# Half 0 of the output projection woven into the last head or pair of two layers of a four-layer trunk

## What is computed

```python
def mla_mixer(h, w_in, q_norm_g, kv_norm_g, w_uq, w_ukv, w_out, cos, sin):    # layer 1, 16 heads
    c_q, c_kv, k_rope, g = split(h @ w_in)
    q, k_nope, v = rmsnorm(c_q) @ w_uq, *(rmsnorm(c_kv) @ w_ukv)     # rotary parts apart
    ...
    p = softmax(where(causal, (q_nope @ k_nope + q_rope @ k_rope) * scale, -inf))
    return ((p @ v) * silu(g)) @ w_out                               # w_out 2048 x 1024
def sb_mixer(h, w_in, w_out):                                        # layer 2, 16 heads of 64
    z = (q @ k) * scale
    log_beta, log_1m_beta = log_sigmoid(z), where(strict, log_sigmoid(-z), 0)
    after = cumsum(log_1m_beta, reverse=True) - log_1m_beta
    a = where(strict, exp(log_beta + after), 0)
    return ((a @ v) * silu(g)) @ w_out                               # w_out 1024 x 1024
```

## Time and profile before

| | |
|---|---|
| median of 3 runs | 2589.19 us |
| lowest, highest | 2583.03, 2590.29 us |
| the profiled execution | 2590.05 us |
| its span in the trace | 2588.1 us |
| mean granted TensorE clock over the span | 0.968 |
| DMA | 160.31 MB, mean 62 GB/s |
| end of the last `pv` of the latent layer | about 1337.7 us |
| end of the last `pv` of stick-breaking | about 2039.9 us |

### The profile page before, as it was taken

The page is one execution under the profiler, slowest core; times in us unless marked ns, Lnnn a source line. Parts: engine busy times, 40 slices in busy tenths (PEclk is TensorE's granted clock), DMA queues, the critical chain, the costliest instruction groups (busy, mean ns, idle before and its releaser), DMA issues. The chain is left out here.

```text
span 2588.1 us, 43259 instructions
## 1 busy us (share of the span) xinstructions
PE 2365.7 (91%) x17364; PEld 1335.5 (52%) x17364; DVE 1569.3 (61%) x2220; ACT 1348.4 (52%) x2029; POOL 462.5 (18%) x418
## 2 busy tenths in 40 slices
PE   8999989987888888989888999999998799999987
PEld 4667654444544454445444455555454345776643
DVE  5566665765655556656546566666666465667654
ACT  4434443445545444444433677777778543444432
POOL 0000111122111102011012223233223210011011
PEclk9999999998899999999989999999999899999998
DMA  3011112214334334424331221121211121111113
GB/s 116 26 42 50 34 34 91 75 48 89 74 75 83 77 79 79 86 65 95 80 86 57 59 58 34 50 58 50 58 41 34 41 91 34 35 50 33 34 59 120
DMA packets 197721, 160.31 MB, mean 62 GB/s; under 512 B 160114, under 2 KB 161394, under 8 KB 197524
## 3 DMA queue, kind: packets, MB, share of 16 engines
q1 hardware_dynamic: 193428, 153.35, 22.4%
q0 software_dynamic: 4096, 4.20, 0.7%
HBM read 98.79 MB, written 4.19 MB: 40 GB/s over the span
## 5 line engine op out<-in xcount | busy, mean ns | idle before, releaser
L240 PE MATMUL psum<-h_hi,w_hi 128*128 128x512 f16 x1128 | 431.7, 383 | 35.7 <-ACT mla_silu_g L285 18.4
L241 PE MATMUL psum<-h_lo,w_hi 128*128 128x512 f16 x1128 | 431.5, 382 | 0.0
L242 PE MATMUL psum<-h_hi,w_lo 128*128 128x512 f16 x1128 | 431.3, 382 | 0.0
L2340 DVE SCALAR_TENSOR_TENSOR w_lo<-wf,w_hi 128x1024 f16<-128x1024 f32 (+3 forms) x194 | 231.1, 1199 | 138.8 <-ACT w_hi L2335 138.7
L256 PE MATMUL psum<-w_hi,h_hi 128*128 128x128 f16 x1504 | 256.9, 219 | 0.0
L258 PE MATMUL psum<-w_hi,h_lo 128*128 128x128 f16 x1504 | 256.5, 219 | 0.0
L257 PE MATMUL psum<-w_lo,h_hi 128*128 128x128 f16 x1504 | 256.5, 219 | 0.0
L1619 ACT ACTIVATE ssum<-psum,mla_neg_top 128x128 f32<-128x128 f32 (+7 forms) x128 | 94.7, 740 | 298.3 <-DVE mla_neg_top L1526 298.3
L1097 POOL TENSOR_TENSOR sb_al<-sb_zc,sb_ah 128x256 f16<-128x256 f32 (+2 forms) x96 | 166.2, 1732 | 373.0 <-ACT sb_ah L1062 373.0
L2335 ACT ACTIVATE w_hi<-wf 128x1024 f16<-128x1024 f32 (+3 forms) x194 | 187.0, 975 | 39.7 <-PE psum L242 19.6
L240 PEld LDWEIGHTS psum<-h_hi,w_hi 128*128 128x128 f16 x1128 | 111.3, 99 | 159.1 <-issue 42.9
(11 more groups left out here) (325 smaller groups left out, 5859.7 us busy)
## 6 DMA issues: line engine op xcount, KB each, us to landing
wf<-in_gla_out SPq DMA_DIRECT2D x32, 512.0 KB, 3.5
wf<-in_sb_in SPq DMA_DIRECT2D x32, 512.0 KB, 3.5
wf<-in_mla_out SPq DMA_DIRECT2D x20, 512.0 KB, 3.9
wf<-in_gla_v SPq DMA_DIRECT2D x16, 512.0 KB, 3.5
wf<-in_gla_g SPq DMA_DIRECT2D x16, 512.0 KB, 3.5
wf<-in_mla_gate SPq DMA_DIRECT2D x16, 512.0 KB, 3.6
wf<-in_sb_out SPq DMA_DIRECT2D x16, 512.0 KB, 3.5
xT<-in_x_T SPq DMA_DIRECT2D x16, 256.0 KB, 5.1
```

What stands on the lines that cost most here:

```text
L240: pe.matmul(out, wh[:, w], act_hi[:, k, tok], start=(i == 0), stop=False)
L241: pe.matmul(out, wh[:, w], act_lo[:, k, tok], start=False, stop=False)
L242: mm = pe.matmul(out, wl[:, w], act_hi[:, k, tok], start=False, stop=(i == last))
L2340: dve.scalar_tensor_tensor(out=self.w_lo[s % Layer.NSPLIT][:, 0:cols], in0=self.wf[s % Layer.NLOAD][:, 0:cols], scalar=W_SCALE, in1=self.w ...
```

## The change

In both layers the eight final output units of half 0 leave the tail for the attention's last head or pair. In the latent layer they stand from block i = 5 of the last head (`OUT_CLOSES`), three of them opened, and all are done ahead of the last `pv`; behind it stand `ns` 0 and then two opened units of half 1. In stick-breaking three units are opened from step 3 of the last pair (`OUT_FROM`) and the rest is woven from step 6 (`HALF_DONE`); one unit of half 1 is opened before the last `pv`, one behind it. The opened units wait for half 0 of the head outputs alone. The squares of half 0 move from ScalarE to GpSimd (`pool_half=0`), and in the latent layer its sums are kept in the tile `st_hi`, since `ssum` is still in use. The latent layer's table puts the norm pieces one unit earlier.

```diff
@@ class Residual
-    def __init__(self, layer, sq):
+    def __init__(self, layer, sq, pool_half=None, rows=None):
...
     def act(self, act, n):
...
-        if not final:
+        if not final or c == self.pool_half:
             return
...
     def pool(self, pool, n):
...
+        s = self.rows[c]
+        if c == self.pool_half:
+            x = L.net.xT[:, k, c * HALF:(c + 1) * HALF]
+            L.wait_unit(pool, n)
+            pool.tensor_tensor(s if k == 0 else self.sq[k % 2], x, x, ALU.mult).then_inc(self.pool_sq_ready, 1)
+            pool.wait_ge(self.pool_sq_ready, k + 1)
+        if k == 0:
+            return
...
         pool.tensor_tensor(s, s, self.sq[k % 2][:], ALU.add).then_inc(self.sum_ready, 1)
@@ class StickBreaking
+    OUT_FROM, HALF_DONE = 3, 6
+    OPENED = 3
...
-            self.resid = Residual(L, [self.zc[0][:, 0, :], self.zc[0][:, 1, :]])
+            self.resid = Residual(L, [self.sg[:, 0, 0:HALF], self.sg[:, 0, HALF:T]], pool_half=0)
@@ def build_items
+                if p == final and i == self.OUT_FROM:
+                    out = []
+                    for k in range(KD):
+                        out += L.slab(w_out[k], 1024, [("x", (k, 0, True))], self.out_banks(k, 0))
+                    filler, out = L.open_early(L.cut(out, ("x",)), self.OPENED)
+                    items += main
+                if p == final and i == self.HALF_DONE:
+                    items += weave(main, filler, lambda it: it[0] == "part")
+                    filler, main = out, []
...
-        early, last = L.open_early(L.cut(last, ("x",)), 2)
-        items += weave(main, early, lambda it: it[0] == "part")
-        items += [("pv", self.PAIRS * len(self.STEPS) - 1)] + last
+        for k in range(KD):
+            last += L.slab(w_out[k], 1024, [("x", (k, 1, True))], self.out_banks(k, 1))
+        first, last = L.open_early(L.cut(last, ("x",)), 1)
+        second, last = L.open_early(last, 1)
+        items += weave(main, filler, lambda it: it[0] in ("u", "part"))
+        items += first + [("pv", self.PAIRS * len(self.STEPS) - 1)] + second + last
@@ def pe
-                pe.wait_ge(self.yl_ready, 2 * (L.share(n, part, KD)[-1] + 1))
+                pe.wait_ge(self.yl_ready, 2 * L.share(n, part, KD)[-1] + c + 1)
@@ class LatentAttention
-            self.resid = Residual(L, [self.rt[0], self.rt[1]])
+            self.resid = Residual(L, [self.rt[0][:], self.rt[1][:]], pool_half=0,
+                                  rows=[self.st_hi[:].bitcast(F32), net.ssum[:, HALF:T]])
...
+    BEHIND = {0: [("nk", 0, 0)], 1: [("nk", 0, 1), ("nk", 0, 2)], 2: [("nk", 0, 3), ("nk", 0, 4)],
+              3: [("nk", 0, 5), ("nk", 0, 6)], 4: [("nk", 0, 7), ("gw", 0)], 5: [], 6: [("gw", 1)]}
+    END = [("gu", 0, 0), ("gw", 2), ("ns", 1)] + Handover.REST
+    OUT_CLOSES = 5
@@ def build_items
-            if i == TT - 1:
+            if h + 1 == MLA_HEADS and i == self.OUT_CLOSES:
+                opened, out = L.open_early(L.cut(self.last_out(0), ("x",)), 3)
+                items += weave_even(main, L.cut(filler, ("x", "g")) + opened, self.pe_cost)
+                main, filler = [], out
+            elif i == TT - 1 and h + 1 < MLA_HEADS:
...
-        early, tail = L.open_early(L.cut(tail, ("x",)), 3)
-        items += early + [("pv", last)] + tail
+        main += [("gap", 2), ("pv", last)]
+        items += weave_even(main, filler, self.pe_cost)
+        early, tail = L.open_early(L.cut(self.last_out(1), ("x",)), 2)
+        items += [("ns", 0)] + early + tail
```

More of the change, by code:

```diff
@@ L353, in __init__ @@
         self.wait_sums, self.wait_slab = wait_sums, wait_slab
+        self.rows = [net.ssum[:, self.half(c)] for c in range(2)]
         self.gain = net.gains[:, coming.gain, :]
@@ L393, in pe @@
                 self.rsqrt.wait_done(pe, 0)
-            pe.matmul(self.bank(c), net.ones[:], net.ssum[:, self.half(c)], start=True,
-                      stop=True).then_inc(self.total, 1)
+            pe.matmul(self.bank(c), net.ones[:], self.rows[c], start=True, stop=True).then_inc(self.total, 1)
         elif kind == "gu":
@@ L549 @@
 class Residual:
-    def __init__(self, layer, sq):
+    def __init__(self, layer, sq, pool_half=None, rows=None):
         L = self.layer = layer
-        self.sq = sq
+        self.rows = rows or [layer.net.ssum[:, c * HALF:(c + 1) * HALF] for c in range(2)]
+        self.sq, self.pool_half = sq, pool_half
         self.sq_ready, self.sum_ready = L.sem("sq_ready"), L.sem("sum_ready")
+        self.pool_sq_ready = L.sem("pool_sq_ready")
     def dve(self, dve, n):
@@ L571, in act @@
         if k == 0:
-            out = L.net.ssum[:, c * HALF:(c + 1) * HALF]
+            out = self.rows[c]
         else:
@@ L587, in pool @@
     def pool(self, pool, n):
-        _, (k, c, final, *_), _, _ = self.layer.units[n]
-        if not final or k == 0:
+        L = self.layer
+        _, (k, c, final, *_), _, b = L.units[n]
+        if not final:
             return
-        s = self.layer.net.ssum[:, c * HALF:(c + 1) * HALF]
-        pool.wait_ge(self.sq_ready, c * KD + k + 1)
+        s = self.rows[c]
[6 more added lines that the diff above has]
+            return
+        if c != self.pool_half:
+            pool.wait_ge(self.sq_ready, (c if self.pool_half is None else 0) * KD + k + 1)
         if k > 1:
@@ L820, in build_items @@
         last = []
-        for c in range(2):
-            for k in range(KD):
-                last += L.slab(w_out[k], 1024, [("x", (k, c, True))], [5, 6, 7])
-        early, last = L.open_early(L.cut(last, ("x",)), 2)
-        items += weave(main, early, lambda it: it[0] == "part")
-        items += [("pv", self.PAIRS * len(self.STEPS) - 1)] + last
+        for k in range(KD):
[4 more added lines that the diff above has]
+        items += first + [("pv", self.PAIRS * len(self.STEPS) - 1)] + second + last
         L.finish_items(self.handover.placed(self.place_products(items), L.units))
@@ L1090, in pool @@
         elif kind == "u":
-            if L.units[a[0]][0] == "x":
+            name, payload, _, _ = L.units[a[0]]
+            if name == "x":
+                if payload[:2] == (1, 0):
+                    pool.wait_ge(self.yt_ready, 2 * (self.PAIRS - 1))
                 self.resid.pool(pool, a[0])
@@ L1191, in __init__ @@
                                      self.wait_out_slab)
+            self.handover.rows = self.resid.rows
+            self.handover.BEHIND, self.handover.END = self.BEHIND, self.END
             self.crs = Rsqrt(L, "latent")
@@ L1323, in build_items, with last_out @@
             main += [("gap", 1)]
[L1324 to L1331 removed]
+        main += [("gap", 2), ("pv", last)]
+        items += weave_even(main, filler, self.pe_cost)
+        early, tail = L.open_early(L.cut(self.last_out(1), ("x",)), 2)
+        items += [("ns", 0)] + early + tail
+        L.finish_items(self.handover.placed(self.place_gates(items), L.units))
+    def last_out(self, c):
+        out = []
+        for part in range(4):
+            out += self.add_units([self.out_slab(MLA_HEADS // self.GROUP - 1, part, (c,))], [0, 0])
+        return out
     def place_gates(self, items):
@@ L1637, in act @@
                                ACT.Copy).then_inc(self.yh_ready, 1)
-    def act_x(self, act, n):
-        k, c, final, group = self.L.units[n][1]
-        if final and (k, c) in ((1, 0), (2, 0)):
-            act.wait_ge(self.rlo, len(self.ropes))
-        self.resid.act(act, n)
     def pool(self, pool, kind, *a):
@@ L1682, in pool @@
         elif kind == "u":
-            if L.units[a[0]][0] == "x":
+            name, payload, _, _ = L.units[a[0]]
+            if name == "x":
+                if payload[:3] == (0, 0, True):
+                    for even_odd in range(2):
+                        pool.wait_ge(self.stacked[even_odd], 256 * (MLA_HEADS // 4))
                 self.resid.pool(pool, a[0])
@@ L2320, in __init__ @@
         self.w_lo_done = ctx.enter_context(nc.semaphore("w_lo_done"))
+        self.queries_staged = [ctx.enter_context(nc.semaphore(f"queries_staged{i}")) for i in range(2)]
         self.guests_from = 0
```

20 lines of the change are left out of this document (9 added, 11 removed).

## The result

| | before | changed |
|---|---|---|
| median | 2589.10 us (4 runs) | 2558.12 us (4 runs) |
| lowest, highest | 2583.03, 2590.29 | 2556.61, 2560.41 |
| the profiled execution, its span | 2590.05, 2588.1 | 2556.61, 2554.9 |
| mean granted clock | 0.968 | 0.977 |

The account below looks back on a forecast made before the run. TensorE, busy 91% of a 2588.1 us span, was taken as the bound. Gains of 17.3 us in stick-breaking and 11.2 in the latent layer made 28.5: 2561.6 profiled, 2560.7 on the median, stated as 2561; range 2546 to 2577.

Parts of the forecast that it names:

- The waits (steps 1, 2, 4 and 6): Stick-breaking's last pair: filled waits +17.9 us, six later matmuls -1.3, step loop longer than TensorE's work -3.5, GpSimd-VectorE interference -2.1.
- Step 6: Stick-breaking: VectorE and GpSimd block each other; two new squares hit a w_lo inside the loop, costing 2.1 us.
- Step 3, the clock: Stick-breaking's last pair and tail: TensorE's slow clock goes, gaining 6.3 us; 1.2 near the first wait stays.
- Step 5: Stick-breaking: GpSimd's `al`, sum and square take 4.7 to 5.2 of 8.4 us per step, so covered.
- Step 1: Latent layer's last head: 69 matmuls (14.9 us) move ahead of the last pv's end, which comes only 7.0 us later.
- Step 2: Latent layer, last pv to last output slab's w_lo: 15.7 us, with half 0's sum matmul waiting 4.2 for GpSimd.
- Step 3: Latent layer, last output slab's w_lo to half 1's sum matmul: one update moves ahead, a 1.64 wait goes; 24.6 us.
- Everything covered: Rival: stick-breaking's step loop hides itself and the latent sums are ready at the last pv's end; 2551 us, chance 0.14.
- The port everywhere: Rival: all 16 squares GpSimd takes over cost 1.07 us each through the port shared with VectorE; 2576, chance 0.10.
- The latent layer gives nothing: Rival: latent head gains turn into the wait at the sum matmul, leaving 17.3 us alone; 2572, chance 0.15.
- Lock-step: Rival: in stick-breaking unit and chain alternate, no wait is filled and the clock falls; slower, 2610 us, chance 0.04.
- It does nothing: Rival: gaps close at one place and open at the next; 2589 us, chance 0.03.

Follow-up runs that it names:

- e5: Changed kernel with six slab splits in stick-breaking's last pair moved behind the next step's subtraction and low half of L; 2556.4 us, 0.9868 of the kernel before.
- e2: Stick-breaking as changed, latent layer as in the kernel before; 2570.7 us, 0.9931 of the kernel before.
- e3: Changed kernel, but in the latent layer half 0's sum matmul stands behind unit 0 of half 1 and norm pieces one unit later, as before; 2560.7 us.
- e7: Changed kernel, but stick-breaking's squares of half 0 are back on ScalarE; 2564.5 us, 0.9901 of the kernel before.
- e9: Changed kernel with half 0's latent sum matmul behind two opened units, second guest slab split later, and stick-breaking's slab splits behind the step; 2552.9 us.
- e8: Changed kernel, but in the latent layer the second guest slab is split behind unit 7 of half 1, not ahead of it; 2559.4 us.
- e1: Latent layer as changed, stick-breaking as in the kernel before; 2580.1 us, 0.9969 of the kernel before.

## Why the prediction was right

The forecast was 28.2 us on the median (2589.2 to 2561); 31.0 came. In the profiled execution 2.1 us lie ahead of P, where nothing was changed, which is luck. The sum of 28.5 for the two places stands against 29.9 measured there if the latent layer is read at Z (9.6 + 20.3), and 31.5 if at C, where the prediction read it (11.2 + 20.3).

**Stick-breaking, 17.3 forecast, 20.3 measured.**
- *The waits (steps 1, 2, 4 and 6)*: 17.9 - 1.3 - 3.5 - 2.1 = 11.0 forecast; TensorE's idle time fell by 11.9. The first wait for L stayed at 2.7 and the six matmuls' 1.3 came, both to the tenth. The loop's regular step was 8.96 us where 9.1 was reckoned, its three waits were 3.3, and e5 took them away and gained 3.2. The price of 3.5 was met with the wrong make-up: TensorE's own step is 8.65 and not 8.4, so a regular step loses 0.3, and the rest falls on the first full-width step and on the one with two slabs. That one took 10.08 us, over the 10 that the prediction gave as a sign of being wrong, and the next made up for it with 6.68.
- *Step 6* was sized too high. Three `w_lo` ahead of a subtraction took 1.33, 1.44 and 1.96 us where 1.23 was reckoned, together 1.0 more and not 2.1, and that is already in the 3.3 of the loop's waits. The largest hit, the `Ll` of 2.28 at 2005.30, shows no price: the step with it took 8.96 us and the next one, without, 8.95.

```profile
2036.87 1.96 DVE L2384 SCALAR_TENSOR_TENSOR w_lo<-wf,w_hi 128x1024 f16<-128x1024 f32 x1 [0.40 <-ACT w_hi L2379]
```

- *Not forecast*: 1.8 for the guests' `w_lo` behind the last output unit; no run here looked into its cause.
- *Step 3, the clock*, was the mis-sized term: 6.3 forecast, 8.4 measured as busy time of the same 599 matmuls. Of this 1.2 is what should have stayed at the first wait. That part is luck of the execution: e2, e3, e7 and e9 lost up to 1.7 there.
- *Step 5*: `al` never came late. It was taken as "covered", and as a cost at most. e7 shows a gain of 4.2, as the squares left the engine whose order is in the loop. Of the forecast's own sum this is no term, since its loop had been written without squares on ScalarE.

**Latent layer, 11.2 forecast, 11.2 measured from P to C, by two errors that cancel.**
- *Step 1* let A move by 7.0; it moved by 4.0 (P to A 45.5 to 49.5). The idle time was sized well: 3.1 of the 4.6 us of leftovers, and 2.8 came, all of it waits for turned probabilities. The 1.5 of slow clock did not come, since all 329 matmuls of the stretch ran at a clock of 1.00, and the slow clock before had cost 1.2 more than the 3.4 reckoned (its three terms add up to 3.3). TensorE's busy time grew by 10.3 for 69 matmuls that take 14.9:

```profile
1290.10:1339.60 49.50, 46.69 (x329) 25.83 (x327) 32.28 (x54) 18.72 (x31) 18.31 (x14) 1.00 0.48 112
```

- *Step 2*, the wait at the sum matmul, was 5.6 for 4.2 forecast. The cause was the one named (GpSimd's square and sum behind the last updates), but not the price: a square took 1.04 and not 1.27 or more, while one square and one sum stood beside VectorE's work and took 2.07 and 2.13. GpSimd needed 11.3 us for the last four units where 10.6 was reckoned, and began 5.7 ahead of A where 6.4 was. The sum matmul itself ran at the slow clock, 2.07 for 1.1. So A to B, up to the `w_lo` below, was 17.9 where 15.7 was forecast.

```profile
1356.11 1.45 DVE L2384 SCALAR_TENSOR_TENSOR w_lo<-wf,w_hi 128x1024 f16<-128x1024 f32 x1 [1.65 <-ACT w_hi L2379]
```

- *Step 3* missed a wait: it let one update go ahead of B and looked no further. The last update went behind the second guest slab's `w_lo`, and the second sum matmul waited 4.9 for it. e8 shows that this place cost 2.9. Yet B to C was 25.4 where 24.6 was forecast, so the rest of that stretch ran about 2 us better than the subtraction of 2.3 had it; which piece did was not tried. A to C was 43.3 where 40.3 was forecast (1385.0 - 1344.7), 2.2 of it from step 2 and 0.8 from step 3.
- *Behind C* nothing was forecast. From C to Z the changed kernel takes 1.6 us more, at a clock of 0.93 where it was 0.99:

```profile
1396.20:1430.50 34.30, 29.02 (x277) 18.80 (x276) 17.28 (x26) 10.96 (x17) 1.67 (x8) 0.99 0.27 67
```

```profile
1382.90:1418.80 35.90, 30.67 (x277) 19.14 (x274) 17.28 (x26) 10.96 (x17) 1.67 (x8) 0.93 0.25 62
```

The same matmuls take 1.6 us more busy time. In e3, where the sum matmul does not wait, C to Z is 34.3 again, but the wait does not settle it: e7 has the same 4.9 us wait and 34.9 at a clock of 0.98, e8 a wait of 2.7 and 35.8 at 0.93. It is clock; what makes it fall there is open.

**The rivals.** *Everything covered* (2551) fell on the waits at L395 and L946. *The port everywhere* (2576): four of the eight squares in stick-breaking took about 2.0 us, but on GpSimd, which has time for them. In the latent layer it has not: the lengthened square and sum stand in the 5.6 us wait, with 1.9 us together by their excess over 1.04 and 1.27 (an estimate). *The latent layer gives nothing* (2572) fell with e1. *Lock-step* (2610): the loop was 8.96 us, far from 13. *It does nothing* is excluded by the interval.

**The signs.** Waits, regular steps and clock in stick-breaking came as announced, the guest wait shrank, and turned probabilities waited less than before. Three signs missed: squares of 1.04 us where 1.3 to 1.7 was given, 5.6 us at the sum matmul for 3 to 5, and the step of 10.08.

## What to carry to other kernels

Where two engines hold each other's next step, list the loop in the order in which each engine takes its instructions, with the work of other streams that stands between: here a slab's split ahead of the subtraction cost 3 us, and a square of 0.6 us a step on the wrong engine 4, though neither VectorE nor ScalarE was near full. Do not stop at the regular step: the uneven ones, at the start and where two slabs fall together, held most of the waits. When work is filled into waits, ask of each instruction that changes its place what now stands behind it, up to the last one of the stage; the last update behind a prefetch's split cost 2.9 us here, more than the sooner norm had brought. And check a piece of a few microseconds at stretches between equal instructions, since what lies ahead of the edit moves by as much, and see how far stretches that were not edited vary too.
